# Two mixing layers of a two-block network: block transposes, key rows and decay tables divided anew between VectorE and ScalarE, and the queries' rotation over four banks

## The reference, cut to what matters

```
# latent attention: 8 heads, 64 plain + 32 rotated columns
q_nope, q_pe = q[..., :MLA_NOPE], rotary(q[..., MLA_NOPE:], positions)
k_nope, v = kv[..., :MLA_NOPE], kv[..., MLA_NOPE:]
k_pe = rotary(kpe, positions)              # one for all heads
s = einsum('bqhd,bkhd->bhqk', qn, k_nope) + einsum('bqhr,bkr->bhqk', qp, k_pe)
p = softmax(s * scale)
o = einsum('bhqk,bkhd->bqhd', p, v)

# retention: decays exp(log_gamma * distance), forward and backward
lg = -exp(log_rate)
dmat = where(mask, exp(lg * maximum(diff, 0.0)), 0.0)
```

## Time and profile before

| | |
|---|---|
| median of 3 runs | 2772.48 us (2771.59 to 2773.01) |
| profiled execution | 2771.85 us, its span 2769.8 us |
| TensorE busy | 2321.4 us, 84% of the span |
| VectorE busy | 846.0 us, 31% |
| ScalarE busy | 380.2 us, 14% |
| granted TensorE clock, mean | 0.921 of full speed |
| layer 0 mixers begin, layer 1 | near 1640 us and 2350 us of the span |

### The profile page before, as it was taken

One profiled execution on the slowest core, in us unless ns is written; L12 is line 12 of the kernel. 1 busy time (PEld: TensorE's weight loads), 2 busy tenths in 40 slices (PEclk: granted clock), 3 DMA queues, 4 the chain that ended last, 5 costly groups with the idle time before them and its releaser, 6 DMA issues. The chain is left out here.

```text
span 2769.8 us, 29357 instructions
## 1 busy us (share of the span) xinstructions
PE 2321.4 (84%) x12064; PEld 1598.8 (58%) x12064; DVE 846.0 (31%) x1584; ACT 380.2 (14%) x854; POOL 6.1 (0%) x11
## 2 busy tenths in 40 slices
PE   8997877566556665666899998999999999899998
PEld 5863752111111111111788885888888888588887
DVE  5345641010000010000543267431034415843001
ACT  2123020000000000000200134210010004231000
POOL 0000000000000000000000000000000000000000
PEclk9997989888887788788999999999999999999999
DMA  9710769999999999999986321086458833105430
GB/s 384 297 73 1 278 262 427 427 427 428 428 428 428 428 428 428 428 427 426 390 302 230 129 84 61 1 335 260 150 209 305 292 128 114 42 21 228 152 122 16
DMA packets 74908, 721.63 MB, mean 261 GB/s; under 512 B 8624, under 2 KB 11696, under 8 KB 13232
## 3 DMA queue, kind: packets, MB, share of 16 engines
q1 hardware_dynamic: 74800, 720.09, 64.4%
HBM read 719.01 MB, written 1.05 MB: 260 GB/s over the span
## 5 line engine op out<-in xcount | busy, mean ns | idle before, releaser
L1543 PE MATMUL bank<-pool 128*128 128x256 f32 x2720 | 596.6, 381 | 6.2 <-ACT pool L1470 6.2
L1543 PEld LDWEIGHTS bank<-pool 128*128 128x128 f32 x2720 | 517.8, 191 | 80.9 <-issue 12.3
L1134 PE MATMUL bank<-pool,moe_x_cur 128*32 128x512 f32 x1792 | 266.5, 731 | 137.7 <-DMA pool<-in_w_expert 137.3
L1575 PE MATMUL bank<-trunk_proj,pool 128*128 128x256 f32 x1408 | 306.4, 380 | 0.0
L1575 PEld LDWEIGHTS bank<-trunk_proj,pool 128*128 128x128 f32 x1408 | 267.1, 190 | 36.0 <-issue 0.8
L1134 PEld LDWEIGHTS bank<-pool,moe_x_cur 128*32 128x32 f32 x1792 | 55.0, 122 | 332.4 <-DMA pool<-in_w_expert 224.2
L1150 PE MATMUL bank<-pool,moe_hidT 128*32 128x512 f32 x896 | 150.3, 807 | 82.6 <-DMA pool<-in_w_expert 75.2
L1761 PE MATMUL bank<-pool 128*128 128x256 f32 x672 | 150.1, 384 | 0.0
L1302 DVE TENSOR_TENSOR moe_hid<-bank,moe_silu 128x512 f32<-128x512 f32 x16 | 11.1, 692 | 448.0 <-ACT moe_silu L1258 448.0
L1761 PEld LDWEIGHTS bank<-pool 128*128 128x128 f32 x672 | 129.4, 193 | 21.4 <-issue 3.8
L1150 PEld LDWEIGHTS bank<-pool,moe_hidT 128*32 128x32 f32 x896 | 29.0, 132 | 183.7 <-DMA pool<-in_w_expert 117.0
(11 more groups left out here) (585 smaller groups left out, 2223.1 us busy)
## 6 DMA issues: line engine op xcount, KB each, us to landing
pool<-in_w_expert SPq DMA_DIRECT2D x168, 2048.0 KB, 35.6
pool<-in_w_ff SPq DMA_DIRECT2D x132, 1024.0 KB, 7.0
pool<-in_w_ada SPq DMA_DIRECT2D x66, 1024.0 KB, 7.1
moe_more<-in_w_expert SPq DMA_DIRECT2D x24, 2048.0 KB, 36.0
pool<-in_w_in SPq DMA_DIRECT2D x40, 1024.0 KB, 4.8
pool<-in_w_mod SPq DMA_DIRECT2D x24, 1024.0 KB, 8.0
pool<-in_w_out SPq DMA_DIRECT2D x10, 1024.0 KB, 10.0
pool<-in_small SPq DMA_DIRECT2D x2, 2560.0 KB, 13.2
```

The source lines that it names most:

```text
L1134: mm = pe.matmul(ps[b][quarter[g], :], x_cur[:, u], w[:, b, g], start=u == 0, stop=u == up_panels - 1)
L1543: mm = pe.matmul(self.ps[p % 3][:, j * T:(j + 1) * T], w[:, j * KD + k], self.hT[:, k], start=k == 0, stop=k == KD - 1)
L1575: mm = pe.matmul(self.ps[3 + q % 2][:, 0:T], w, x[:, k], start=k == 0, stop=k == nk - 1)
```

## The change

It does the following, the same in both layers.

- **Turning back.** One transpose over all 128 partitions writes the turned blocks to `flat_blocks`; four ScalarE copies (32 partitions, 512 elements each, read with a stride) carry them onto the diagonals of `z`. `z_twice` is gone.
- **Key rows.** ScalarE, no longer VectorE, copies the 32 key rows for eight heads.
- **Decay tables.** ScalarE makes the first half of each (`ahead` times `lg`, L2171 before) behind the copies. VectorE's second half (L2173) moves into the level steps, after n = 1, 2, 4, 5; ScalarE's exponential (L1990) follows after its work of n = 3, 4, 6, 7, with the sign as its scale, so L2168 is gone. The two pieces of `between` at n = 4, 5 move to 6, 7.
- **Rotation.** The swaps use banks 5, 6, 3, 4. Swap 2 and 3 wait for ScalarE's copies of the values, not for VectorE, and stand behind `in_pair(10)`. VectorE forms each pair's sum at once.
- **Waits.** The score tiles of the first units use banks 0, 1, 3, 2 and wait accordingly; `tensor_beside` waits for `by_sin` 2 in place of 4 and for the key rows; ScalarE waits for its own four copies ahead of the first exponential.

```diff
@@ -1666,9 +1666,10 @@
+        swap_bank = lambda p: ps[(5, 6, 3, 4)[p]]
...
@@ -1854,14 +1855,16 @@
 
-            for p in range(4):
-                if p < 2:
-                    pe.wait_ge(k_out, 3 + p)
-                else:
-                    pe.wait_ge(by_sin, p - 1)
-                pe.matmul(ps[5 + p % 2][0:96, 0:2 * T], cst["swap_mla"][0:96, 0:96], b["q"][:, 2 * p:2 * p + 2],
+            def swap_q(p):
+                pe.wait_ge(*((k_out, 3), (k_out, 4), (value_out, 1), (value_out, 2))[p])
+                pe.matmul(swap_bank(p)[0:96, 0:2 * T], cst["swap_mla"][0:96, 0:96], b["q"][:, 2 * p:2 * p + 2],
                           start=True, stop=True).then_inc(q_swapped, 1)
+
+            swap_q(0)
+            swap_q(1)
             in_pair(10)
+            swap_q(2)
+            swap_q(3)
             beside_last(pe)
...
@@ -1984,10 +1987,21 @@
                 sc.activation(b["l_values"][:, t], ps[3 + t], ACT.Copy).then_inc(value_out, 1)
+            sc.wait_ge(kpe_raised, 1)
+            sc.activation(b["k"][HEAD:96], ps[7][HEAD:96, 0:T].unsqueeze(1).broadcast_to([32, 8, T]), ACT.Copy)\
+                .then_inc(kpe_out, 1)
+            sc.wait_ge(substituted, 1)
+            sc.wait_ge(cleared, 3)
+            for q in range(4):
+                part = slice(32 * q, 32 * q + 32)
+                sc.activation(b["z"][part, :, :, part],
+                              flat_blocks[part].rearrange("p (t o g j) -> p o g j t", o=2, g=4, j=4)[:, 0], ACT.Copy)\
+                    .then_inc(z_out, 1)
+            sc.wait_ge(small_here, 32)
+            sc.wait_ge(lg_made, 1)
+            for h in range(4):
+                sc.activation(decay[h], cst["ahead"], ACT.Identity, scale=lg[:, h:h + 1]).then_inc(spread_ahead, 1)
             pair_out(10)
-            for h in range(4):
-                sc.wait_ge(spread, 2 * h + 2)
-                sc.activation(decay[h], decay[h], ACT.Exp).then_inc(decayed, 1)
             beside_last(sc)
...
@@ -2159,34 +2173,17 @@
                     latent_scale(1)
-            ve.wait_ge(cleared, 3)
-            for q in range(4):
-                part = slice(32 * q, 32 * q + 32)
-                ve.transpose(b["z_twice"][part, part, :, 0:16],
-                             x_blocks[part].rearrange("p s t -> p t s")).then_inc(substituted, 1)
-            ve.wait_ge(lg_made, 1)
-            link(ve.tensor_scalar(lg, lg, -1.0, None, MUL))
-            ve.wait_ge(small_here, 32)
-            for h in range(4):
-                ve.tensor_scalar(decay[h], cst["ahead"], lg[:, h:h + 1], None, MUL).then_inc(spread, 1)
-                ve.wait_ge(spread, 2 * h + 1)
-                ve.scalar_tensor_tensor(decay[h], cst["behind"], lg[:, 4 + h:5 + h], decay[h], MUL, ADD).then_inc(spread, 1)
-            ve.wait_ge(kpe_raised, 1)
-            ve.tensor_copy(b["k"][HEAD:96], ps[7][HEAD:96, 0:T].unsqueeze(1).broadcast_to([32, 8, T]))
+            ve.transpose(flat_blocks, x_blocks.rearrange("p s t -> p t s")).then_inc(substituted, 1)
             wide = lambda x: x.unsqueeze(1).broadcast_to([96, 2, T])
             for p in range(4):
                 tiles = slice(2 * p, 2 * p + 2)
                 ve.wait_ge(q_swapped, p + 1)
-                ve.tensor_tensor(b["turned"][:, tiles], ps[5 + p % 2][0:96].rearrange("p (a b) -> p a b", b=T),
+                ve.tensor_tensor(b["turned"][:, tiles], swap_bank(p)[0:96].rearrange("p (a b) -> p a b", b=T),
                                  wide(tables[0:96, 1, 1]), MUL).then_inc(by_sin, 1)
                 ve.tensor_tensor(b["q"][:, tiles], b["q"][:, tiles], wide(tables[0:96, 1, 0]), MUL).then_inc(by_cos, 1)
-            for p in range(4):
-                tiles = slice(2 * p, 2 * p + 2)
                 ve.wait_ge(by_sin, p + 1)
                 ve.wait_ge(by_cos, p + 1)
                 ve.tensor_tensor(b["q"][:, tiles], b["q"][:, tiles], b["turned"][:, tiles], ADD).then_inc(q_ready, 1)
-
-
...
@@ -2788,7 +2785,7 @@
-        score_bank = lambda u: ps[(0, 3, 1, 2)[u % 4]]
+        score_bank = lambda u: ps[(0, 1, 3, 2)[u % 4]]
...
@@ -2829,14 +2826,15 @@
 
-                pe.wait_ge(*((enter.in_out, 10), (enter.value_out, NT), (enter.in_out, 11), (enter.in_out, 12))[u])
+                pe.wait_ge(*((enter.in_out, 10), (enter.in_out, 11), (enter.by_sin, 3), (enter.in_out, 12))[u])
             pe.matmul(score_bank(u)[:, 0:T], b["q"][:, h, t * P:(t + 1) * P], b["k"][:, h], start=True, stop=True)\
                 .then_inc(scored, 1)
 
         def tensor_beside(pe):
 
             pe.wait_ge(enter.in_out, 10)
-            pe.wait_ge(enter.by_sin, 4)
+            pe.wait_ge(enter.by_sin, 2)
+            pe.wait_ge(enter.kpe_out, 1)
             for j in range(2):
...
@@ -2847,6 +2845,8 @@
                     pe.wait_ge(copied, u - 1)
+                else:
+                    pe.wait_ge(enter.by_sin, 4)
                 for j in range(NT):
...
@@ -2879,7 +2879,7 @@
-                    pe.wait_ge(exped, 14)
+                    pe.wait_ge(exped, 15)
...
@@ -2911,7 +2911,7 @@
-                    pe.wait_ge(enter.substituted, 4)
+                    pe.wait_ge(enter.z_out, 4)
...
@@ -3131,6 +3131,7 @@
+            sc.wait_ge(enter.z_out, 4)
...
@@ -3181,6 +3182,10 @@
                     x_out(n + 2)
+                if n in (3, 4, 6, 7):
+                    h = (3, 4, 6, 7).index(n)
+                    sc.wait_ge(spread, h + 1)
+                    sc.activation(decay[h], decay[h], ACT.Exp, scale=-1.0).then_inc(decayed, 1)
...
@@ -3275,11 +3280,16 @@
                     ve.tensor_tensor(bonus, ps[7].rearrange("p (a b) -> p a b", b=T), vv, MUL).then_inc(bonus_out, 1)
-                if n == 4:
+                if n in (1, 2, 4, 5):
+                    h = (1, 2, 4, 5).index(n)
+                    ve.wait_ge(enter.spread_ahead, h + 1)
+                    ve.scalar_tensor_tensor(decay[h], cst["behind"], b["lg"][:, 4 + h:5 + h], decay[h], MUL, ADD)\
+                        .then_inc(spread, 1)
+                if n == 6:
                     ve.wait_ge(bonus_out, 1)
                     for j in range(2):
                         ve.scalar_tensor_tensor(bonus[:, j], bonus[:, j], v("ln_b", j), y_gate[:, j], ADD, MUL)
-                if n == 5:
+                if n == 7:
                     for j in range(2):
```

More of the change, by code:

```diff
@@ L1668, in __init__ @@
             st.sem(n) for n in ("gate_made", "gate_out", "v_turned", "v_copied", "halves", "exped", "q_ready"))
-        prepared, tri_made, tri_copied, cleared, substituted, lg_made, spread, decayed = (
-            st.sem(n) for n in ("prepared", "tri_made", "tri_copied", "cleared", "substituted", "lg_made", "spread",
-                                "decayed"))
+        prepared, tri_made, tri_copied, cleared, substituted, z_out, lg_made, spread_ahead, kpe_out = (
+            st.sem(n) for n in ("prepared", "tri_made", "tri_copied", "cleared", "substituted", "z_out", "lg_made",
+                                "spread_ahead", "kpe_out"))
+        swap_bank = lambda p: ps[(5, 6, 3, 4)[p]]
         tri_bank = lambda half, e: ps[((3, 4), (7, 6))[e][half]]
@@ L2199, in __init__ @@
         self.sync, self.tensor, self.scalar, self.vector, self.gpsimd = sync, tensor, scalar, vector, gpsimd
-        self.substituted, self.decayed = substituted, decayed
+        self.z_out, self.spread_ahead, self.kpe_out = z_out, spread_ahead, kpe_out
         self.load_vec, self.vec_here, self.side_load, self.side_panel = load_vec, vec_here, side_load, side_panel
@@ L2749, in __init__ @@
             "told", "rhs_out", "solved", "negated", "carried", "state_made", "read"))
-        ret_scored, weighted, ret_mixed, out_made, out_added = (sem(n) for n in (
-            "ret_scored", "weighted", "ret_mixed", "out_made", "out_added"))
+        spread, decayed, ret_scored, weighted, ret_mixed, out_made, out_added = (sem(n) for n in (
+            "spread", "decayed", "ret_scored", "weighted", "ret_mixed", "out_made", "out_added"))
         ret_out, y_by_act, y_by_dve, meaned, centred, squared, summed, rooted = (sem(n) for n in (
@@ L3296, in vector @@
                     .then_inc(negated, 1)
-                ve.wait_ge(enter.decayed, s + 1)
+                ve.wait_ge(decayed, s + 1)
                 ve.wait_ge(ret_scored, s + 1)
@@ L3365, in mixer_buffers @@
     b["z"] = ring[:, mark:mark + 8 * T].rearrange("p (a b c) -> p a b c", a=4, b=4)
-    b["z_twice"] = ring[:, mark:mark + 32 * T].rearrange("p (o m s) -> p s o m", o=2, s=P)
     b["flat_blocks"] = ring[:, mark + 8 * T:mark + 12 * T]
```

## The result

| | before | with the change |
|---|---|---|
| median | 2772.64 us (2771.59 to 2773.01, 4 runs) | 2748.71 us (2746.91 to 2749.39, 4 runs) |
| profiled execution, its span | 2771.85 us, 2769.8 us | 2749.26 us, 2747.3 us |

The ratio is 0.9913, with a 95% interval of 0.9896 to 0.993. The change makes the kernel 23.9 us faster; 25.3 us were forecast, and 2747.2 us.

What follows compares the result with a forecast made beforehand. VectorE's queue was taken to bound the place, with TensorE waiting. 27.66 us gained less 2 x 0.4 (loop) and 2 x 0.8 (levels) gave 25.3 us, so 2747.2 us was forecast, range 2744 to 2754 us.

Steps and rivals of the forecast that it cites:

- What bounds the place: Around the swaps in layer 0: VectorE's queue bounds, TensorE waits 11.13 us and is slow afterwards, ScalarE is free.
- the lower clock's part: Share of the 27.66 us gain put down to TensorE's slower clock after its pause in layer 0: 1.4 us.
- TensorE's own sum: Swap 0 to third score tile without waits: 16.65 us, gaining 14.22 us in layer 0 and 13.44 in layer 1.
- What hides ScalarE's work: Under pair 10: ScalarE's key rows, copies onto z and decay-table halves stay hidden, with 4 us to spare.
- the turning point: Cost of each strided ScalarE copy onto z above which TensorE would wait: 1.6 us, against 0.6 us assumed.
- The loop's start: First score tiles: late rotation, then the exponential's table load, lose 0.4 us a layer; bounds nothing and 1.5 us.
- The level steps: Table load and exponentials among ScalarE's copies exceed its idle time, delaying the output projection by 0.8 us a layer.
- the full price: Rival, level steps: all 3.5 us of load and exponentials lost in each layer, result 2752.6 us; chance 0.15.
- The strided copies: Rival, copies onto z: 2.22 us each, second score tile waits 2.1 us a layer, result 2751.4 us; chance 0.07.
- second load time: Rival, ScalarE's table switches: running empty costs another 1.28 us per load, 2.6 us lost, result 2749.8 us; chance 0.08.
- The change did what it says: Opposite of a rival: TensorE's pause only moves behind the pair, time unchanged at 2772.5 us; chance 0.03.
- The sum: Whole kernel: 27.66 us gained, less 2 x 0.4 and 2 x 0.8, makes 25.3 us.

Runs made afterwards that it cites:

- the relief alone: The changed kernel with the rotation as before the change (two banks, all four swaps ahead of pair 10, swaps 2 and 3 waiting for VectorE's sines): 2743.26 us.

## Why the prediction was right, point by point

**What bounds the place: right.** VectorE's list held TensorE. With the relief alone the pause goes, with the new rotation alone 4.68 us of it stay. One reading was too small: I put the lower clock's part in layer 0 at 1.4 us, from `in_pair(10)` alone. Swaps 2 and 3 ahead of it also ran behind the pause, in 3.52 us from start to start where they take 1.72 with the change, so the clock's part was 3.2 us. The sum does not hang on this, since it takes the whole distance from swap 0 to the third tile.

**TensorE's own sum: right, 0.27 us too large.** I had 16.65 us from swap 0 to the third tile; it is 16.38 and 16.39. I took `in_pair(10)` at the length of its group, 7.07 us, though the next group starts 0.16 us before that group's end, and each two swaps at 1.77 us, which take 1.72.

**What hides ScalarE's work: right in its outcome, one term mis-sized.** The key rows took 1.87 us (2.4 as the upper bound), the copies 1.1 us each (0.6, inside the bounds of 0.60 and 2.22 us), the halves of the tables 0.64 us (0.55). Pair 10's copy came at 1684.25, 9.77 us from swap 0, while I had 8.8; TensorE wants it 12.5 us from swap 0. I had put the turning point at 1.6 us a copy. With the copies doubled they took 8.95 us and TensorE waited 2.26 us, so 6.69 us were covered, 1.67 us a copy: close to that point.

**The loop's start: mechanism right, size 0.4 for 0.91 us.** The third maximum follows its tile by 1.54 us, not 0.63. The step that failed is the difference of two nearly equal times, VectorE free at 17.7 us from swap 0 and the tile ready at 17.3. VectorE was free at 17.92, since each sum waits for its cosine and starts 0.78 us behind it, not 0.6 (1684.78 to 1685.56). The tile was ready at 17.01, by TensorE's own shorter sum. Two errors of 0.2 and 0.3 us doubled the term. ScalarE's copy of `in_pair(11)` stands behind the two late exponentials, which I had not followed: TensorE waits 0.62 us for it ahead of the fourth tile. That wait is hidden, since VectorE comes to this tile only after the third.

**The level steps: right.** 0.71 us a layer, 0.8 forecast, by the load and exponentials that exceed ScalarE's idle time. That the size came so close is partly luck, since two errors cancel. From start to start the load and the three exponentials took 3.20 us and not 2.93, and the five copies between them 2.05 us where they had taken 2.36 without the idle time. TensorE idles for only 0.30 us of the delay, ahead of a second product. Before, that second product (L2952) started while the last records of the first one (L2937) still ran; now it starts behind them. The rule of the Trainium skill (ScalarE: Activation LUTs, What ACT_TABLE_LOAD costs), by which a switch would cost 1.38 us of drain beside the 1.28 us, would have made it 2.2 us, an estimate from that page's figure. The trace does not agree: from 1734.95 to 1736.24 the load takes 1.29 us to the next instruction's start, it starts 0.02 us after the end of the one before, and taking it away together with four exponentials gives back 0.71 us.

**The rivals.** The levels paid 0.71 of the 3.5 us of the full price. The strided copies were slow, 1.1 us instead of 0.6, but under the turning point, so nothing of it came out. No second load time showed ahead of a table switch. The change did what it says.

**The sum.** The two stages gained 24.7 us against 25.3: TensorE's sum gave 0.5 us more than reckoned, the loop cost 1.0 us more, the levels 0.2 us less, and 0.2 us more was lost behind them. The median gained 23.9 us. What I had no term for is the clock behind the barrier, 1.3 us; the sentence that the stage's end moves with everything else was wrong by that. It is within what single executions differ by, but it stands in all five profiles with the change's loop start and level steps. That the median came within 1.5 us of the forecast rests on the stages; of the rest, the first block alone moves single executions by more.

## What to carry to other kernels

When one engine waits at the end of another's list, the parts that shorten the list and those that fill the pause compete for the same microseconds: measured apart they gave 12.4 to 13.2 and about 7.3 us a layer, together 12.0 to 12.8. Once the list is short, see whether the filling still pays; here putting it back to its old place, ahead of the pair, gave 0.9 us a layer. Look for a place where the table of an activation function is loaded anyway: here the exponentials cost nothing there, and 0.7 us a layer between the copies of a three-engine chain.

## What I had not expected of the hardware

- A block transpose on VectorE took about as long over 32 partitions as over 128, at 1024 columns each: 2.22 us for one of the four of before, 1.94 us for the one of the change, and 1.96 us for the earlier one (L2151). The four also wrote to every second column, so the 0.3 us between them need not come from the partitions, and other column counts were not measured.
- ScalarE reading every 32nd float32 took 1.1 us for 512 elements, and 0.64 us for 512 neighbouring ones, both written in runs of 32.
- What a pause of TensorE costs afterwards did not grow with its length. Swaps 2 and 3 with `in_pair(10)` take 8.63 us from start to start with the change. Behind a pause of 11.1 us (before) they took 11.82 us in layer 0 and 11.06 in layer 1, behind one of 4.1 us (turning back alone) 12.01 and 11.22. Behind 2.26 us (copies doubled) the next pair lost nothing in one layer and 1.7 us in the other, in one and the same execution. Behind the barrier's pause of 3.6 to 3.7 us three levels appear; only the change was profiled twice, and both times it had 0.63.
